# Moving the matmul operands of a 3-block transformer kernel by 32 and 64 bytes in SBUF

## The chip, the cores and the metric

The kernel runs on one core of one Trainium2 chip. The metric is the device time of one execution in microseconds (us); lower is better. SBUF, the on-chip memory, has 128 partitions; an address in this document is a byte or word offset along a partition, the same in all 128. A word is 4 bytes. TensorE multiplies a **moving** operand (up to 512 columns, streamed through) with a **stationary** operand (up to 128 columns, put into the array by a separate weight-load instruction). Both are read from SBUF, and the result is added up in PSUM.

## The reference, cut to what matters

256 tokens of width 2048 pass through three transformer blocks. The projections hold nearly all of the arithmetic:

```
# twice: mixer, then a gated feed-forward (FFN_HIDDEN = 5632)
h = mixer(x @ w_in, ...) @ w_o
x = layer_norm(ALPHA * x + h)
gate, up = jnp.split(x @ w_gu, 2, axis=-1)
x = layer_norm(ALPHA * x + (silu(gate) * up) @ w_d)
# once: neighbourhood + state-space + memory attention, then D_FF = 8192
x = x + rmsnorm(y @ w_out)
x = x + rmsnorm(square(relu(rmsnorm(x) @ w_ff1)) @ w_ff2)
```

All of it is float32. The kernel reaches float32 accuracy with a split: each operand is a high part, rounded to the `float32r` form that TensorE multiplies at a higher rate, plus a low part that holds the rest. A product is then three matmuls: high by high, high by low, low by high.

## The kernel before

**Units.** A weight matrix comes in units of 1024 words for each partition (512 KB). Each lands in one of 8 slots of `weights_raw` (or in a place in the large buffer), ScalarE copies its high part to a slot of `weights_hi` (L294), VectorE subtracts and writes the low part to `weights_lo` (L313), and TensorE uses it. There are 4 slots in each of the two, and one more of each in the large buffer (`hi_at[4]`, `lo_at[4]`).

**Matmuls.** In `block_mm` (L353 to L355) the weights are the moving operand, 512 columns at a time, and the activations are the stationary one, 128 tokens at a time. For each 128 rows of the weight matrix and each of the two token blocks, three matmuls follow one another:

```
nc.tensor.matmul(o, ah, wh, start=(k + j == 0), stop=False)
nc.tensor.matmul(o, ah, wl, start=False, stop=False)
last = nc.tensor.matmul(o, al, wh, start=False, stop=(k + j == kts - 1))
```

The first argument after the output is the stationary operand, the second the moving one. `ah` and `al` are slices of `act_hi`/`act_lo` (all the projections from the model width) or of `hid_hi`/`hid_lo` (the down projections). The same triple stands at L3972 to L3974 (gated feed-forward: here some activations lie in the large buffer, rows "weights_hi,big"), at L693 to L695, L608 to L610 and L580 to L582. Names in the profile's rows are in the order output<-moving,stationary. `narrow_mm` (L382 to L384) has the roles turned round: 16 or 72 weight columns are stationary and 256 tokens of `act_hi`/`act_lo` move. Small attention products (L1046, L3666 and others) and transposes by an identity (L413) are plain float32.

**Addresses.** `build` lays all of SBUF out by hand, in words: `weights_hi` at 8192, `weights_lo` at 12288, `x` at 16384, and from `SCR` = 20480 on `act_hi`, `act_lo`, `hid_hi`, `hid_lo`. `scr(...)` gives other views of those last four, used in other stages. Behind them stand `ident`, `smalls` and the large buffer `BIG`, of which `big(...)` gives views by offset. Every weight slot, every 512-column half of one, and every 128-column slice of the activations begins a multiple of 128 words after that layout's start. So in every triple the stationary and the moving operand have the same address modulo 512 bytes.

**Order.** The order of the work on every engine is written out by hand. Semaphores order the engines: `lo_ready` lets TensorE use a unit, `w_used` gives a slot of the split weights back, and a load into a raw slot waits for `lo_ready` of the unit that was there.

Of the kernel before, what the change touches and what calls it, by code (L numbers as in the profile page):

```python
# [19 lines left out]
F32R = mybir.dt.float32r  # L20
I32 = mybir.dt.int32
# [4 lines left out]
P = 128  # L26
TOK = 256
TT = TOK // P
D = 2048
KT_D = D // P  # L30
# [147 lines left out]
def build(nc, A, out, upto=99):  # L178
# [4 lines left out]
    def at(name, word, shape, dt=F32):  # L183
        assert base + 4 * (word + int(np.prod(shape[1:]))) <= nc.sbuf_usable_end, name
        return nc.alloc_sbuf_tensor_at(name, shape, dt, offset=base + 4 * word)
# [7 lines left out]
    w_lo = at("weights_lo", 12288, [P, SPLIT_SLOTS, UNIT], F32R)  # L193
    x = at("x", 16384, [P, TT, D])
    SCR = 20480
    aT_hi = at("act_hi", SCR, [P, KT_D, TOK], F32R)
    aT_lo = at("act_lo", SCR + 4096, [P, KT_D, TOK], F32R)
    hT_hi = at("hid_hi", SCR + 8192, [P, 8, TOK], F32R)
    hT_lo = at("hid_lo", SCR + 10240, [P, 8, TOK], F32R)
    CON = SCR + 12288  # L200
    ident = at("ident", CON, [P, P])
    smalls = at("smalls", CON + 128, [P, 128])
    BIG = CON + 256
    BIG_END = 53200
    n_view = [0]

    def scr(off, shape, dt=F32):
        n_view[0] += 1
        assert off + int(np.prod(shape[1:])) <= 12288
        return at(f"scratch_{n_view[0]}", SCR + off, shape, dt)  # L210

    def big(off, shape, dt=F32):
        n_view[0] += 1
        assert BIG + off + int(np.prod(shape[1:])) <= BIG_END
        return at(f"big_{n_view[0]}", BIG + off, shape, dt)
# [547 lines left out]
    gdec = big(19856, [P, 16])  # L763
    restart = big(17152, [P, 1024])
    dil_mask = big(18176, [P, 1152])
    chunk_pred = big(20048, [P, P], I32)
    G_Q, G_K, G_V, G_G, G_R, D_Q, D_K, D_V = 0, 512, 1024, 2048, 2064, 3088, 4624, 6160

    ln_vec = [[big(o, [P, D]), big(o + D, [P, D])] for o in (12544, 10752, 10912, 10240)]
# [165 lines left out]
    b_glu = big(18432, [P, 512])  # L935
    mlp_post = big(2048, [P, D])
    dump = scr(8192, [P, TT, D])
    still = scr(8192, [P, P])
    GJ = 32
    T4 = 4  # L940
# [14 lines left out]
    dmat = big(18432, [P, 16, T4 * 16])  # L955
    u4x = big(8192, [P, 16, 2, NCH])
    ux = scr(8192, [NCH, GJ, T4, 16])
    hs = scr(8192, [P, NCH, 2, GJ])
    y4 = big(8192, [NCH, 4, T4, P])
# [3203 lines left out]
def program(nc, shapes, dtypes, upto=99):  # L4163
    aps = {n[3:]: nc.dram_tensor(n, shapes[n], dtypes[n], kind="ExternalInput").ap() for n in shapes}
    out = nc.dram_tensor("out_x", (1, TOK, D), F32, kind="ExternalOutput").ap()
    build(nc, aps, out, upto)
# [86 lines left out]
```

How the kernel before makes its waits and increments, by code:

```python
    def slot_load(sp, c, slot, src, cols, unit):  # L262
        nk = src.shape[1]
        if slot in c.user:
            sp.wait_ge(lo_ready, c.until(c.user[slot] + 1))
        sp.dma_start(raw_at[slot][:, :nk * cols].rearrange("p (k n) -> p k n", n=cols), src).then_inc(landed[slot], 16)
        c.n[f"raw{slot}"] += 1
        c.use(slot, unit)
# [7 lines left out]
    def unit_hi(act, c, size):  # L277
        slot = c.raw_slot()
        act.wait_ge(landed[slot], c.now(f"raw{slot}", 1, 1, 16))
        c.n[f"raw{slot}"] += 1
        high_part(act, c, raw_at[slot], size)
# [1 line left out]
    def high_part(act, c, of, size):  # L285
        to = c.split_slot()
        if to in c.user:
            act.wait_ge(w_used, c.until(c.user[to] + 1))
        done = 0
        if c.n["unit"] == 0:
            done = UNIT // 2
            nc.scalar.copy(hi_at[to][:, :done], of[:, :done]).then_inc(ready("tile_high"), 1)
        nc.scalar.copy(hi_at[to][:, done:size], of[:, done:size]).then_inc(hi_ready, 1)
        c.use(to, c.n["unit"])
        c.n["split"] += 1
        c.n["unit"] += 1
# [5 lines left out]
    def low_part(dve, c, of, size):  # L303
        to = c.split_slot()
        done = 0
        if c.n["unit"] == 0:
            done = UNIT // 2
            dve.wait_ge(ready("tile_high"), 1)
            nc.vector.tensor_tensor(lo_at[to][:, :done], of[:, :done], hi_at[to][:, :done].bitcast(F32),
                                    ALU.subtract).then_inc(ready("tile_low"), 1)
        dve.wait_ge(hi_ready, c.now("unit", 1))
```

## Time and profile before

| | |
|---|---|
| median of 3 runs | 3403.22 us (3403.2 to 3405.02) |
| the profiled execution's own time | 3405.52 us |
| its span, from the first to the last instruction | 3403.7 us |
| TensorE (matmul) busy | 3387.6 us, 100% of the span |
| granted TensorE clock, mean | 0.999 of full speed |
| matmul records | 15664 |
| VectorE, ScalarE busy | 2225.6 us (65%), 1737.9 us (51%) |
| HBM traffic | 184 GB/s over the span |

The span is 1.8 us shorter than the execution's own time. Matmul records overlap: one lasts longer than the distance from its start to the start of the next. So the rate of TensorE is read from starts, not from durations.

### The profile page before, as it was taken

Reading aid. Unit: us, or ns where it says so; the run is one execution under the profiler, and the core shown is the slowest. Engines: PE = TensorE matmul, PEld = TensorE weight load, DVE = VectorE, ACT = ScalarE, POOL = GpSimd, SP = SyncE. Lnnn points to the kernel's source line nnn. Section 1 sums busy time; section 2 is a strip of 40 time slices with the busy share of each in tenths; the row PEclk is TensorE's granted clock in tenths of the full one; section 3 lists DMA queues with packets and bytes.
Section 4 is the critical chain, followed back from the end, with each engine's and each line's share of the span. In section 5 each row is a group of like instructions: output and inputs, shape, how many; then the busy total and the mean of one; then the engine's idle time right before and its main releaser. Section 6 shows DMA issues by size and latency. Waiting matters only on the chain.

```text
span 3403.7 us, 41843 instructions
## 1 busy us (share of the span) xinstructions
PE 3387.6 (100%) x15664; PEld 2774.5 (82%) x15664; DVE 2225.6 (65%) x2428; ACT 1737.9 (51%) x2211; POOL 302.4 (9%) x418
## 2 busy tenths in 40 slices
PE   9999999999999999999999999999999999999998
PEld 8788878888888887777888878888888788888887
DVE  4544477888887755666556545557544887777776
ACT  5444445555554455454444434446546665555553
POOL 0000000000000000002343303000281000000000
PEclk9999999999999999999999999999999999999999
DMA  7556555665666465456666657665654466665654
GB/s 246 170 167 182 192 185 180 210 211 173 213 210 205 148 185 156 126 196 170 188 186 196 189 161 211 212 194 172 181 182 147 143 223 198 198 197 195 196 186 130
DMA packets 333339, 630.42 MB, mean 185 GB/s; under 512 B 33180, under 2 KB 36096, under 8 KB 331648
## 3 DMA queue, kind: packets, MB, share of 16 engines
q1 hardware_dynamic: 326272, 603.20, 56.5%
q0 software_dynamic: 6768, 25.05, 2.3%
q8 instruction: 102, 1.67, 0.2%
q14 instruction: 53, 0.43, 0.0%
q10 hardware_dynamic: 144, 0.07, 0.0%
HBM read 624.86 MB, written 2.33 MB: 184 GB/s over the span
## 4 chain that ended last, share of the span: by engine, by line
PE 96%; DVE 2%; ACT 1%; DMA 0%; issue 0%; SPq 0%; DVEq 0%; ACTq 0%
PE psum L353 23%; PE psum L355 22%; PE psum L354 22%; PE psum L3974 6%; PE psum L3972 6%; PE psum L3973 6%; PE psum L413 3%; PE psum L693 1%; PE psum L1046 1%; PE psum L695 1%; PE psum L694 1%; DVE weights_lo L313 1%; PE psum L1059 0%; PE psum L3869 0%; PE psum L610 0%; PE psum L608 0%
## 5 line engine op out<-in xcount | busy, mean ns | idle before, releaser
L313 DVE TENSOR_TENSOR weights_lo<-weights_raw,weights_hi 128x1024 fp32r<-128x1024 f32 (+1 forms) x1069 | 1315.2, 1239 | 932.4 <-ACT weights_hi L294 926.9
L294 ACT CAST weights_hi<-weights_raw 128x1024 fp32r<-128x1024 f32 (+1 forms) x1069 | 1118.9, 1049 | 1351.6 <-PE psum L355 1163.3
L353 PE MATMUL psum<-weights_hi,act_hi 128*128 128x512 f32 x2088 | 834.0, 399 | 0.2
L355 PE MATMUL psum<-weights_hi,act_lo 128*128 128x512 f32 x2088 | 815.8, 391 | 0.0
L354 PE MATMUL psum<-weights_lo,act_hi 128*128 128x512 f32 x2088 | 814.1, 390 | 0.0
L353 PE MATMUL psum<-weights_hi,hid_hi 128*128 128x512 f32 x1192 | 467.6, 392 | 0.2 <-DVE big L3214 0.2
L355 PE MATMUL psum<-weights_hi,hid_lo 128*128 128x512 f32 x1192 | 464.3, 389 | 0.0
L354 PE MATMUL psum<-weights_lo,hid_hi 128*128 128x512 f32 x1192 | 463.9, 389 | 0.0
L353 PEld LDWEIGHTS psum<-weights_hi,act_hi 128*128 128x128 f32 x2088 | 392.7, 188 | 86.0 <-issue 8.9
L355 PEld LDWEIGHTS psum<-weights_hi,act_lo 128*128 128x128 f32 x2088 | 392.3, 188 | 84.7
L354 PEld LDWEIGHTS psum<-weights_lo,act_hi 128*128 128x128 f32 x2088 | 393.1, 188 | 76.4
L353 PEld LDWEIGHTS psum<-weights_hi,hid_hi 128*128 128x128 f32 x1192 | 223.8, 188 | 48.7 <-issue 2.7
L355 PEld LDWEIGHTS psum<-weights_hi,hid_lo 128*128 128x128 f32 x1192 | 223.7, 188 | 47.1
L354 PEld LDWEIGHTS psum<-weights_lo,hid_hi 128*128 128x128 f32 x1192 | 223.9, 188 | 45.5
L3972 PE MATMUL psum<-weights_hi,act_hi 128*128 128x512 f32 x478 | 187.4, 392 | 0.0
L3974 PE MATMUL psum<-weights_hi,act_lo 128*128 128x512 f32 x478 | 186.3, 390 | 0.0
L3973 PE MATMUL psum<-weights_lo,act_hi 128*128 128x512 f32 x478 | 186.0, 389 | 0.0
L294 ACT CAST big<-weights_raw 128x1024 fp32r<-128x1024 f32 x100 | 105.3, 1053 | 92.0 <-PE psum L3974 47.3
L313 DVE TENSOR_TENSOR big<-weights_raw,big 128x1024 fp32r<-128x1024 f32 x100 | 122.2, 1222 | 32.7 <-ACT big L294 32.4
L413 PE MATMUL psum<-ident,big 128*128 128x128 f32 (+1 forms) x754 | 117.3, 272 | 0.2 <-DVE hid_lo L430 0.2
L413 PEld LDWEIGHTS psum<-ident,big 128*128 128x128 f32 (+1 forms) x754 | 93.4, 139 | 28.9 <-issue 3.5
L2391 DVE TENSOR_TENSOR x<-x,psum 128x1024 f32<-128x1024 f32 x54 | 65.8, 1219 | 60.4 <-PE psum L355 60.4
(523 smaller groups left out, 3751.3 us busy)
## 6 DMA issues: line engine op xcount, KB each, us to landing
weights_raw<-in_ffn_wgu SPq DMA_DIRECT2D x312, 512.0 KB, 4.0
weights_raw<-in_w_ff SPq DMA_DIRECT2D x224, 512.0 KB, 4.7
weights_raw<-in_ffn_wd SPq DMA_DIRECT2D x176, 512.0 KB, 4.4
weights_raw<-in_even_w_in SPq DMA_DIRECT2D x120, 512.0 KB, 3.6
weights_raw<-in_w_in SPq DMA_DIRECT2D x64, 512.0 KB, 3.8
weights_raw<-in_odd_w_in SPq DMA_DIRECT2D x60, 512.0 KB, 3.7
big<-in_ffn_wgu SPq DMA_DIRECT2D x32, 512.0 KB, 8.1
weights_raw<-in_odd_w_o SPq DMA_DIRECT2D x32, 512.0 KB, 3.7
```

The lines of the kernel that those rows point to most:

```text
L294: nc.scalar.copy(hi_at[to][:, done:size], of[:, done:size]).then_inc(hi_ready, 1)
L313: nc.vector.tensor_tensor(lo_at[to][:, done:size], of[:, done:size], hi_at[to][:, done:size].bitcast(F32), ALU.subtract).then_inc(lo_ready, 1)
L353: nc.tensor.matmul(o, ah, wh, start=(k + j == 0), stop=False)
L354: nc.tensor.matmul(o, ah, wl, start=False, stop=False)
L355: last = nc.tensor.matmul(o, al, wh, start=False, stop=(k + j == kts - 1))
L413: last = nc.tensor.transpose(psum[:w, 4 + t % 2, at_col:at_col + p], src, ident[:p, :p])
L693: nc.tensor.matmul(o, ah, wh, start=(u + j == 0), stop=False)
L694: nc.tensor.matmul(o, ah, wl, start=False, stop=False)
L2391: return TENS(o, o, s, ALU.add)
L3972: nc.tensor.matmul(at_bank(b), ah, wh, start=start_, stop=False, skip_group_check=True)
L3973: nc.tensor.matmul(at_bank(b), ah, wl, start=False, stop=False, skip_group_check=True)
L3974: last = nc.tensor.matmul(at_bank(b), al, wh, start=False, stop=stop, skip_group_check=True)
```

## The change

Offsets in SBUF, and nothing else. `act_hi` moves up by 8 words (32 bytes). `act_lo`, `hid_hi`, `hid_lo`, `ident`, `smalls`, the whole large buffer and the views of `scr` move up by 16 words (64 bytes). The weight slots (`weights_raw`, `weights_hi`, `weights_lo`) and `x` stay. `chunk_pred`, a mask in the large buffer, takes an offset 144 words lower so that the buffer still ends inside SBUF. No instruction is added, removed or put in another place; the sequence on every engine is the same.

```diff
-    aT_hi = at("act_hi", SCR, [P, KT_D, TOK], F32R)
-    aT_lo = at("act_lo", SCR + 4096, [P, KT_D, TOK], F32R)
-    hT_hi = at("hid_hi", SCR + 8192, [P, 8, TOK], F32R)
-    hT_lo = at("hid_lo", SCR + 10240, [P, 8, TOK], F32R)
-    CON = SCR + 12288
+    aT_hi = at("act_hi", SCR + 8, [P, KT_D, TOK], F32R)
+    aT_lo = at("act_lo", SCR + 4096 + 16, [P, KT_D, TOK], F32R)
+    hT_hi = at("hid_hi", SCR + 8192 + 16, [P, 8, TOK], F32R)
+    hT_lo = at("hid_lo", SCR + 10240 + 16, [P, 8, TOK], F32R)
+    CON = SCR + 12288 + 16
     ident = at("ident", CON, [P, P])
     smalls = at("smalls", CON + 128, [P, 128])
     BIG = CON + 256
@@
-        return at(f"scratch_{n_view[0]}", SCR + off, shape, dt)
+        return at(f"scratch_{n_view[0]}", SCR + 16 + off, shape, dt)
@@
-    chunk_pred = big(20048, [P, P], I32)
+    chunk_pred = big(19904, [P, P], I32)
```

After the change the stationary operand stands 32 bytes (`act_hi`) or 64 bytes (`act_lo`, `hid_hi`, `hid_lo`, activations in the large buffer) further than the moving one, modulo 512 bytes, where the moving one is a slot of `weights_hi` or `weights_lo`. Where the moving operand is the weight slot in the large buffer, it moves too: against `hid_hi`, `hid_lo`, `act_lo` and `big` the distance stays 0, against `act_hi` it becomes -32 bytes. In `narrow_mm` the moving operand (`act_hi`, `act_lo`) moves and the stationary one stays.

## Rows read from the trace of the kernel before

**Rows 1.** The page: busy time, TensorE's clock in 40 slices, the chain by engine.

```profile
PE 3387.6 (100%) x15664; PEld 2774.5 (82%) x15664; DVE 2225.6 (65%) x2428; ACT 1737.9 (51%) x2211; POOL 302.4 (9%) x418
...
PEclk9999999999999999999999999999999999999999
...
PE 96%; DVE 2%; ACT 1%; DMA 0%; issue 0%; SPq 0%; DVEq 0%; ACTq 0%
```

**Rows 2.** Matmul groups by line and shape: count, busy us, mean ns of one, idle before.

```profile
L353 PE MATMUL psum<-weights_hi,act_hi 128*128 128x512 f32 x2088 | 834.0, 399 | 0.2
...
L353 PE MATMUL psum<-weights_hi,hid_hi 128*128 128x512 f32 x1192 | 467.6, 392 | 0.2 <-DVE big L3214 0.2
...
L3972 PE MATMUL psum<-weights_hi,act_hi 128*128 128x512 f32 x478 | 187.4, 392 | 0.0
...
L3972 PE MATMUL psum<-weights_hi,big 128*128 128x512 f32 x222 | 88.7, 400 | 0.0
...
L353 PE MATMUL psum<-big,hid_hi 128*128 128x512 f32 x128 | 49.9, 390 | 0.0
...
L3972 PE MATMUL psum<-big,act_hi 128*128 128x512 f32 x122 | 47.7, 391 | 0.0
...
L3972 PE MATMUL psum<-big,big 128*128 128x512 f32 x78 | 30.7, 394 | 0.0
...
L3666 PE MATMUL psum<-big,big 128*128 128x256 f32 x24 | 5.8, 380 | 0.0
```

**Rows 3.** Timeline, TensorE, us from 297: start and duration of single matmuls.

```profile
297.13 0.39 PE L353 MATMUL psum<-weights_hi,act_hi 128*128 128x512 f32 x1
...
310.73 0.39 PE L353 MATMUL psum<-weights_hi,act_hi 128*128 128x512 f32 x1
```

**Rows 4.** Timeline, TensorE, us 221 to 225, behind and ahead of transposes.

```profile
221.86 0.40 PE L354 MATMUL psum<-weights_lo,act_hi 128*128 128x512 f32 x1
222.09 0.40 PE L355 MATMUL psum<-weights_hi,act_lo 128*128 128x512 f32 x1
222.32 0.40 PE L353 MATMUL psum<-weights_hi,act_hi 128*128 128x512 f32 x1
222.56 0.39 PE L354 MATMUL psum<-weights_lo,act_hi 128*128 128x512 f32 x1
222.78 0.39 PE L355 MATMUL psum<-weights_hi,act_lo 128*128 128x512 f32 x1
...
223.94 0.39 PE L354 MATMUL psum<-weights_lo,act_hi 128*128 128x512 f32 x1
...
224.40 0.60 PE L413 MATMUL psum<-ident,big 128*128 128x128 f32 x4
```

**Rows 5.** Weight loads by line and shape: count, busy us, mean ns, idle before.

```profile
L353 PEld LDWEIGHTS psum<-weights_hi,act_hi 128*128 128x128 f32 x2088 | 392.7, 188 | 86.0 <-issue 8.9 <-DVE weights_lo L313 0.9
...
L382 PEld LDWEIGHTS psum<-act_hi,weights_hi 128*72 128x72 f32 x16 | 2.3, 141 | 0.0
...
L382 PEld LDWEIGHTS psum<-act_hi,weights_hi 128*16 128x16 f32 x16 | 1.5, 94 | 0.4
```

**Rows 6.** Timeline, TensorE, us 56 to 60: `narrow_mm` with 16 stationary columns.

```profile
56.01 0.28 PE L382 MATMUL psum<-act_hi,weights_hi 128*16 128x256 f32 x1
...
59.88 0.28 PE L382 MATMUL psum<-act_hi,weights_hi 128*16 128x256 f32 x1
```

**Rows 7.** Timeline, weight loads, at us 297.

```profile
297.13 0.19 PEld L354 LDWEIGHTS psum<-weights_lo,act_hi 128*128 128x128 f32 x1
```

**Rows 8.** Timeline, TensorE, us 327: plain float32 matmuls of 256 columns.

```profile
327.71 1.46 PE L3666 MATMUL psum<-big,big 128*128 128x256 f32 x6
```

**Rows 9.** Waits: who waited for whom, us in total, times, longest.

```profile
ACT weights_hi L294 <- PE psum L355: 1203.7, 746, 6.3
```

**Rows 10.** DMA issues: count, KB each, median us from issue to landing.

```profile
weights_raw<-in_ffn_wgu SPq DMA_DIRECT2D x312, 512.0 KB, 4.0
...
big<-in_ffn_wgu SPq DMA_DIRECT2D x32, 512.0 KB, 8.1
```

## The prediction

> **What bounds the kernel now.** I read the page first. TensorE is busy for the whole span, its clock is granted in full in every slice, and the chain that ended last is TensorE for 96% [rows 1]. So a change of the time has to be a change of TensorE's rate, or a new wait. Next comes what it does. The groups by line show three equal rows for every triple (high by high, high by low, low by high), of which one stands here: 2088 + 1192 + 478 + 222 + 128 + 122 + 78 = 4308, times 3 is 12,924 matmuls of 512 columns [rows 2]. A few smaller groups of the same kind I leave out. The durations of 389 to 400 ns say nothing about the rate, since one matmul starts before the last has ended. The timeline gives it: from the L353 at 297.13 to the L353 at 310.73 lie 20 triples, 60 starts, in 13.60 us [rows 3]. That is 226.7 ns for each matmul, and 12,924 x 0.2267 = 2930 us, 86% of the span.
>
> At 2.4 GHz, one column a cycle, 512 columns are 213.3 ns. So each matmul pays 13.4 ns on top, 173 us in all. Whatever these 13.4 ns are, the change can act on nothing else: TensorE has no idle time worth naming, and no instruction moves.
>
> **What the change can touch.** It changes addresses alone. The term is 12,924 times the change of one interval, so 0.53 ns for each matmul is already 6.8 us, the 0.2% that a measurement of this kernel can tell from no change. The question is whether the 13.4 ns come from two reads of SBUF that stand in each other's way: the stream of the moving operand, and the weight load for the next matmul. The two do overlap: the matmul L353 starts at 297.13, and the weight load for the following L354 starts at 297.13 as well [rows 3, 7]. And before the change both start at the same address modulo 512 bytes.
>
> *For a collision.* The interval isn't a constant. Behind a group of transposes it goes 0.23, 0.23, 0.24, 0.22 us, and from 221.86 to 223.94 nine starts take 2.08 us, 231.1 ns each, before it settles at 226.7 [rows 3, 4]. The operands are of the same kind in both stretches, so the same work costs 4.4 ns more or less by how loads and streams lie in time. A plain float32 matmul of 256 columns, which takes two cycles for each column and so also streams for 213.3 ns, has less on top: six of them last 1.46 us, and less the last one's own 0.380 that is 1.08 / 5 = 216 ns [rows 2, 8]. It reads SBUF at half the rate and would have room for a second reader.
>
> *Against a collision that the address decides.* In `narrow_mm` the moving side is again `float32r`, 256 columns, ideally 106.7 ns. Between 56.01 and 59.88 lie 33 starts in 3.87 us, 117.3 ns each [rows 6]. The load there is 16 columns, an eighth of a full one, and the slices are 64 bytes apart, so that the distance between the two operands runs through eight values modulo 512 bytes. The cost on top is still 10.6 ns. So at most 13.4 - 10.6 = 2.8 ns of the 13.4 go with the size of the load, and over those eight distances the pace keeps even to what the timeline resolves. Second, the two reads don't run side by side. A load lasts 94, 141 and 188 ns for 16, 72 and 128 columns [rows 5], which is (188 - 94) / 112 = 0.84 ns a column, against 226.7 / 512 = 0.44 for the stream. While the load walks through its 512 bytes, the stream walks through some 1000, so the distance between them sweeps through about 500 bytes in every matmul. A shift of 32 or 64 bytes moves the point in the sweep where they meet, not how often they do.
>
> So I take 0 for the term, and keep as its bounds -10.7 ns (down to the 216 of the plain float32 matmul) and +4.4 ns (up to the 231.1 behind the transposes), for each of 12,924 matmuls: -138 us and +57 us.
>
> The Trainium skill ("SBUF — State Buffer", section "Who interferes with whom") says that TensorE reads the moving operand and the weight load through two independent ports, and that PE and ACT never wait on anyone. By that rule the term is 0 as well. The same page ("Specifications") names lines of 16 bytes; 32 and 64 are multiples of 16, so no operand would touch more lines than before. But the skill ("TensorE: Matmul & The Clock Gate", section "Back-to-back issue gap") gives N / 2.4 + 2.5 ns for a warm matmul, 215.8 for 512 columns, and the trace's 226.7 doesn't agree; if the change brought the interval to that figure, the time would be an estimated 141 us shorter. No run here says yet where the difference comes from.
>
> **The rest of the edits** I cost at nothing. The views in `big` and `scr` that VectorE, ScalarE and GpSimd use move by 64 bytes; VectorE is busy for 65% and ScalarE for 51% [rows 1], and ScalarE waits 1203.7 us in 746 waits, 1.6 each, for TensorE to give weight slots back [rows 9]. That slack hides some tenths more on an instruction. Units that land in the large buffer take 8.1 us against 4.0 in a raw slot [rows 10]; both ways they are issued ahead, and if the new destination made one slower by those 4 us again, ScalarE's slack would be gone for that unit: 32 such units and at worst 4 - 1.6 = 2.4 us each, 77 us. I see nothing that would do it, since the size and the shape of each transfer stay.
>
> The sum is 0 on the profiled execution, whose own time is 3405.5 for a span of 3403.7, 2.3 above the median of the runs. Against that median I forecast 3403.
>
> **The rivals.**
>
> *A, faster: the distance between the operands matters.* The part that goes with the load, 2.8 ns, would vanish: 12,924 x 2.8 = 36 us, 3367 us. If the whole excess over 216 were a collision, it would be 3265. For it: the interval answers to fine timing [rows 3, 4], and in every triple the distance was exactly 0 before, the one value of which a sweep can't be shown to be harmless, for no full-width load at another distance stands beside a `float32r` stream in the groups. Against it: `narrow_mm` and the sweep. 0.32 for this side, most of it near the small end.
>
> *B, slower: the settled rhythm is lost.* The stream settles at 226.7 with load and stream starting together [rows 3, 7]. With other addresses the meeting point lies elsewhere, and high and low stationary operands now differ from one another (32 and 64 bytes), so that the triple may not settle and stays at the 231.1 seen behind transposes [rows 4]. That is 12,924 x 4.4 = 57 us, 3460. Half of it, if only one of the three in a triple and its neighbour suffer, is 3432. It decides as soon as the mean interval grows by 0.53 ns. Against it: that it needs the same sensitivity to addresses as A, and then in the worse direction. 0.18.
>
> *C, the change does nothing,* because the 13.4 ns belong to each `float32r` matmul whatever its addresses are: my forecast, 0.50, with a range of its own of 3400 to 3408.
>
> **How the numbers follow.** C is the likeliest and gives 3403. A reaches down to 3265, B up to 3460. I let the range end at 3350, which holds A's small form and leaves some 0.12 below it, and at 3425, which holds a B of 1.7 ns a matmul and leaves some 0.07 above. Faster by over 0.2% is A, 0.32; within 0.2% is C, 0.50; slower by over 0.2% is B, 0.18.
>
> **What the changed kernel's profile would show.** If I am right: the same 60 starts of L353 to L355 in 13.60 us, the same 33 starts of L382 in 3.87, the same duration of weight loads, 188 ns. If A: fewer than 13.57 us for 60 starts of rows with `weights_hi` against `act_hi` and `hid_hi`, while the rows "big,hid_hi" [rows 2], in which both operands move by 64 bytes, stay at 226.7; that difference would prove the distance and not the address. If B: more than 13.63 us, and the uneven steps of [rows 4] all through a block. I would be wrong also if the weight loads themselves changed their length, or if a wait for a DMA into the large buffer appeared in the chain.

## The result: slower by 1.7%

The changed kernel takes 3462.88 us (median of 4 runs, 3462.34 to 3463.4) against 3403.89 us for the kernel before in the same comparison (3403.2 to 3405.02): 59.0 us more, a ratio of 1.0173 with a 95% interval of 1.0155 to 1.0191. The forecast was no change.

The page of the profiled execution after the change, its head, the busy line, TensorE's clock and the chain by engine:

```profile
span 3460.9 us, 41843 instructions
...
PE 3446.1 (100%) x15664; PEld 2772.1 (80%) x15664; DVE 2225.5 (64%) x2428; ACT 1736.1 (50%) x2211; POOL 302.1 (9%) x418
...
PEclk9999999999999999999999999999999999999999
...
PE 98%; DVE 1%; ACT 1%; issue 0%; DVEq 0%; POOL 0%; ACTq 0%; POOLq 0%
```

Beside [rows 1] nothing has moved but TensorE: the same 15,664 matmuls at the same clock, granted in full, take 57 us more of the span (3460.9 against 3403.7), and VectorE, ScalarE and the weight loads are as busy as before. So the loss is TensorE's pace. The timeline of TensorE after the change: `narrow_mm`, which answers to [rows 6], the stretch that answers to [rows 3] (`act_hi`, `act_lo` stationary), and one with `hid_hi`, `hid_lo`:

```profile
56.25 0.28 PE L382 MATMUL psum<-act_hi,weights_hi 128*16 128x256 f32 x1
...
60.10 0.28 PE L382 MATMUL psum<-act_hi,weights_hi 128*16 128x256 f32 x1
...
297.24 0.39 PE L355 MATMUL psum<-weights_hi,act_lo 128*128 128x512 f32 x1
...
311.12 0.39 PE L355 MATMUL psum<-weights_hi,act_lo 128*128 128x512 f32 x1
...
709.50 0.39 PE L353 MATMUL psum<-weights_hi,hid_hi 128*128 128x512 f32 x1
...
716.50 0.39 PE L353 MATMUL psum<-weights_hi,hid_hi 128*128 128x512 f32 x1
```

From the first row to the second of a stretch, 60 starts take 13.88 us, 231.3 ns each, where they took 13.60 before [rows 3]. In the down projection 30 starts take 7.00 us, 233.3 ns each. `narrow_mm` keeps its pace: 33 starts in 3.85 us, 3.87 before [rows 6]. The matmul groups by line of the changed kernel:

```profile
L353 PE MATMUL psum<-weights_hi,act_hi 128*128 128x512 f32 x2088 | 839.0, 402 | 0.1
...
L353 PE MATMUL psum<-weights_hi,hid_hi 128*128 128x512 f32 x1192 | 473.3, 397 | 0.0
...
L353 PE MATMUL psum<-big,hid_hi 128*128 128x512 f32 x128 | 50.1, 391 | 0.0
```

The first two rows grew from 399 and 392 ns [rows 2]. The third, in which both operands moved by 64 bytes, has 391 against 390. A duration isn't a pace, though: by their starts these `hid_hi` matmuls went from 226.7 to 229.0 ns, in the midst of neighbours at a distance of 64 bytes, where the matmuls of `weights_hi` and `weights_lo` against `hid_hi` went from 227.0 to 233.3.

The sum of it: (2088 + 478) x 3 = 7698 matmuls with `act_hi`/`act_lo` and a weight slot x 4.6 ns = 35 us; 1192 x 3 = 3576 with `hid_hi`/`hid_lo` x 6.6 = 24 us; 222 x 3 = 666 with activations in the large buffer x 6.6 = 4 us. That is 63 us by settled paces. Added up from every start in the two traces, the 57.2 us between the spans are 28.0 for `act_hi`/`act_lo` against a weight slot (8177 matmuls, some of them in rows that the sum leaves out), 22.0 for `hid_hi`/`hid_lo` (3624), 3.5 for activations in the large buffer (666) and 3.8 where the moving operand isn't one of the plain weight slots (1176). The other 2020 matmuls, narrow ones, transposes and plain float32, lost 0.0. The first two shares are smaller than by settled paces, since the kernel before wasn't settled everywhere either [rows 4]: its matmuls with `act_hi`/`act_lo` took 227.8 ns on average, not 226.7, leaving out intervals of 250 ns and more.

### The profile page after: what moved, and what is told of

It reads as the page before. It is cut to its first block, busy times and chain, and to the rows that moved or that the text cites. A ratio compares the mean times of both kernels' runs of the same rounds, so it can differ in the third digit from the quotient of the medians.

```text
span 3460.9 us, 41843 instructions
## 1 busy us (share of the span) xinstructions
PE 3446.1 (100%) x15664; PEld 2772.1 (80%) x15664; DVE 2225.5 (64%) x2428; ACT 1736.1 (50%) x2211; POOL 302.1 (9%) x418
## 3 DMA queue, kind: packets, MB, share of 16 engines
q8 instruction: 102, 1.67, 0.2%
## 4 chain that ended last, share of the span: by engine, by line
PE 98%; DVE 1%; ACT 1%; issue 0%; DVEq 0%; POOL 0%; ACTq 0%; POOLq 0%
PE psum L353 23%; PE psum L354 23%; PE psum L355 23%; PE psum L3972 6%; PE psum L3973 6%; PE psum L3974 6%; PE psum L413 3%; PE psum L693 1%; PE psum L1046 1%; PE psum L694 1%; PE psum L695 1%; PE psum L610 0%; PE psum L609 0%; PE psum L608 0%; PE psum L1059 0%; PE psum L3869 0%
## 5 line engine op out<-in xcount | busy, mean ns | idle before, releaser
L354 PE MATMUL psum<-weights_lo,act_hi 128*128 128x512 f32 x2088 | 823.2, 394 | 0.0
L3973 PE MATMUL psum<-weights_lo,act_hi 128*128 128x512 f32 x478 | 188.2, 394 | 0.0
```

What stands on the lines that cost most here:

```text
L3973: nc.tensor.matmul(at_bank(b), ah, wl, start=False, stop=False, skip_group_check=True)
```

## The experiments

The theory that I set out with: the distance between the stationary and the moving operand, modulo some power of two, sets the pace of a `float32r` matmul. The rivals: the move of the activations or of the large buffer counts by itself (other alignment for transfers or for the other engines); or high and low operands at two distances keep the triple from settling.

### Everything moved together (all_moved), and one distance for all (apart_32, apart_64, apart_96)

All four in one comparison, in which the kernel before took 3403.35 us (9 runs). all_moved keeps the offsets of before and moves the start of the whole layout:

```diff
-    base = -(-nc.sbuf_base // 64) * 64
+    base = -(-nc.sbuf_base // 64) * 64 + 64
...
-    chunk_pred = big(20048, [P, P], I32)
+    chunk_pred = big(19904, [P, P], I32)
```

The other three are the change with one number N (8, 16 or 24 words) in all its places; apart_96 also lets the layout end 8 words later:

```diff
-    aT_hi = at("act_hi", SCR, [P, KT_D, TOK], F32R)
-    aT_lo = at("act_lo", SCR + 4096, [P, KT_D, TOK], F32R)
+    aT_hi = at("act_hi", SCR + N, [P, KT_D, TOK], F32R)
+    aT_lo = at("act_lo", SCR + 4096 + N, [P, KT_D, TOK], F32R)
...
-    CON = SCR + 12288
+    CON = SCR + 12288 + N
```

> Every tensor in SBUF moves up by 64 bytes, the weight slots too, so every address differs from the kernel before but every distance between a stationary and a moving operand is what it was, 0 modulo 512 bytes. Distance theory (the distance between the operands sets the pace of a float32r matmul): 3403 us, settled interval 226.7 ns. Address theory (where the activations, the scratch views or the large buffer lie, by themselves, sets the time): 3463 us, settled interval near 233 ns.

> All that stands behind the weight slots and x (activations, scratch views, constants, large buffer) is 32 bytes further; one distance for high and low operands alike. Distance theory: rows with distance 32 take some 230.6 ns, as the matmuls of the change whose own and next stationary operand both stand at 32 do, so 12,300 x 3.9 ns = 48 us more than before, 3451 us. Mixture theory (the triple can't settle because high and low operands stand at different distances, 32 and 64): one distance settles at 226.7, 3403 us.

> As apart_32, with 64 bytes for everything. Distance theory: all rows go like the hid rows of the change, 233.3 ns, so 12,300 x 6.6 ns = 81 us more than before, 3484 us, slower than the change itself. Mixture theory: 3403 us.

> As apart_32, with 96 bytes for everything. Distance theory has no number for 96 from the two traces: slower than before if 0 is a special point, and between 226.7 and 236 ns for a matmul, so 3403 to 3520 us. Mixture theory: 3403 us.

| kernel | distance of the activations from the weight slots | median, us (runs) | ratio, 95% interval |
|---|---|---|---|
| all_moved | 0 | 3404.65 (8) | 1.0003 (0.9991 to 1.0014) |
| apart_32 | 32 bytes | 3473.42 (2) | 1.0205 (1.0176 to 1.0235) |
| apart_64 | 64 bytes | 3475.08 (2) | 1.021 (1.018 to 1.024) |
| apart_96 | 96 bytes | 3482.99 (2) | 1.0233 (1.0204 to 1.0263) |

The timeline of TensorE in apart_64, behind the first starts of a block:

```profile
300.18 0.39 PE L355 MATMUL psum<-weights_hi,act_lo 128*128 128x512 f32 x1
...
311.38 0.39 PE L355 MATMUL psum<-weights_hi,act_lo 128*128 128x512 f32 x1
```

48 starts in 11.20 us are 233.3 ns each. Every address in all_moved is new, 64 bytes higher, and it costs nothing, so the new addresses by themselves are out. One distance for high and low alike costs more than the two of the change, so the mixture is out too, and the forecast's own reason for the slow rival with it. The distance theory stands, but its number for 32 bytes was wrong: I had read 230.6 ns from those matmuls of the change that stand among neighbours at 64, and a kernel all at 32 runs at 233.2 on average. A pace belongs to a sequence of distances, not to one matmul. For apart_64 I had expected 81 us more and it was 72: the settled 6.6 ns were taken for every matmul, though not all of them ran at 226.7 before.

### A map of the distance (distance_map)

A kernel of its own, which leaves out the whole computation and only issues matmuls from data at rest, while all the other engines are idle (a cut of it; the comments are added here):

```
            for i in range(reps // 3):
                k = i % 2
                ah, al = hi[:, 128 * k:128 * k + width], lo[:, 256 + 128 * k:256 + 128 * k + width]
                wh, wl = w[:, 0:cols], w[:, 512:512 + cols]
                mm(ah, wh, cols, width)
                mm(ah, wl, cols, width)
                last = mm(al, wh, cols, width)
...
        for g in GAPS:            # 0, 8, 16, 32, 48, 64, 96, ... 480, 496 bytes
            part(still[g], still[g], moving)
```

> Not the reference's computation: this kernel leaves all of it out and only issues matmuls. 20 groups of 96 float32r matmuls of 512 columns, in the same triples as the kernel before, each group behind four plain float32 matmuls; within a group the stationary operands stand at one distance from the moving ones modulo 512 bytes, from 0 to 496. Then the pair of distances of the change (high 32, low 64), loads of 16 and 64 columns at distances 0 and 64, matmuls of 256 columns at 0 and 64, and bf16 at 0, 64 and 256. Distance theory: group 0 takes 226.7 ns a matmul once settled (96 in 21.9 us), groups 32 and 64 some 233 (22.5 us), group 96 some 234. A variant in which memory is split in banks by a few low address bits: the pace repeats with a period (64, 128 or 256 bytes) and is 226.7 again there. A variant in which only the same address is special: every other distance takes 230 ns or more. If the stream and the load collide at all, loads of 16 columns lose less with the distance than loads of 128, and bf16 matmuls, which read half the bytes, show no difference between the distances and come nearer to 213.3.

Its timeline on TensorE, one row for a group of 96 matmuls: start, then the time from the first start to the last end. The name of the stationary operand says the distance.

```profile
137.47 22.64 PE L72 MATMUL psum<-moving,gap064b 128*128 128x512 f32 x96
...
184.13 22.55 PE L72 MATMUL psum<-moving,gap128b 128*128 128x512 f32 x96
...
230.62 22.23 PE L72 MATMUL psum<-moving,gap192b 128*128 128x512 f32 x96
...
276.79 22.05 PE L72 MATMUL psum<-moving,gap256b 128*128 128x512 f32 x96
...
322.77 22.65 PE L72 MATMUL psum<-moving,gap320b 128*128 128x512 f32 x96
...
369.44 22.55 PE L72 MATMUL psum<-moving,gap384b 128*128 128x512 f32 x96
...
415.92 22.23 PE L72 MATMUL psum<-moving,gap448b 128*128 128x512 f32 x96
...
508.00 22.43 PE L72 MATMUL psum<-moving,gap000b 128*16 128x512 f32 x96
...
531.08 22.48 PE L72 MATMUL psum<-moving,gap064b 128*16 128x512 f32 x96
...
600.39 11.76 PE L72 MATMUL psum<-moving,gap000b 128*128 128x256 f32 x96
...
612.80 11.55 PE L72 MATMUL psum<-moving,gap064b 128*128 128x256 f32 x96
...
625.08 20.88 PE L72 MATMUL psum<-moving_b,bf000b 128*128 128x512 bf16 x96
646.69 20.88 PE L72 MATMUL psum<-moving_b,bf064b 128*128 128x512 bf16 x96
```

To read a pace off a row, take away the last one's own 0.39 us and divide by the 95 intervals: 22.05 gives 228.0 ns, 22.64 gives 234.2. The first starts of a group weigh in there. The settled pace, from the starts of the last 48 matmuls of a group in the trace, by the distance modulo 256 bytes:

| distance, bytes | 0 | 32 | 64 | 96 | 128 | 160 | 192 | 224 | 240 |
|---|---|---|---|---|---|---|---|---|---|
| settled ns | 226.7 | 233.3 | 233.3 | 234.3 | 232.4 | 233.3 | 228.9 | 233.3 | 228.3 |

The pairs 64 and 320, 128 and 384, 192 and 448 are equal to within 0.01 us in 22: over the 20 distances tried the pace repeats after 256 bytes. 0 (and 256) is the best of the 20 distances. The paces agree with the kernel's, 226.7 at 0 and 233.3 at 64, with the other engines at rest, so VectorE, ScalarE and the transfers have no part in it. bf16 takes 215.8 ns settled at each of its three distances, the rows are alike to 0.01 us; so of the two types only `float32r` shows the effect. Whether its twice as many bytes are the reason isn't shown: its weight loads last longer too, 193 ns against 98 for bf16, and plain float32 is in no map. With loads of 16 columns the distance hardly counts, 231.1 ns at 0 and 231.7 at 64. That much was expected. Two things weren't. With loads of 16 columns instead of 128, distance 0 takes 231.1 ns, more than with full loads. And with 256 moving columns distance 0 is the slower one: 120.0 ns settled against 117.8 at 64.

### The map tried on the kernel (acts_first_minus_64)

The map says that 64 bytes the other way cost less. The activations are laid out ahead of the weight slots, and all behind them moves:

```diff
-    w_hi = at("weights_hi", 8192, [P, SPLIT_SLOTS, UNIT], F32R)
-    w_lo = at("weights_lo", 12288, [P, SPLIT_SLOTS, UNIT], F32R)
-    x = at("x", 16384, [P, TT, D])
-    SCR = 20480
+    SCR = 8192
+    w_hi = at("weights_hi", SCR + 12288 + 16, [P, SPLIT_SLOTS, UNIT], F32R)
+    w_lo = at("weights_lo", SCR + 16384 + 16, [P, SPLIT_SLOTS, UNIT], F32R)
+    x = at("x", SCR + 20480 + 16, [P, TT, D])
...
-    CON = SCR + 12288
+    CON = SCR + 24576 + 16
```

> All of the kernel before, with the activations laid out ahead of the weight slots and the weight slots, x and the rest 64 bytes further: the activations now stand at distance -64 (192 modulo 256) from the weight slots. Distance theory with the period of 256 bytes from the distance map: 228.9 ns a matmul at 192 against 226.7 at 0, on some 12,000 matmuls, so 27 us more than before, 3430 us. If any distance but 0 costs the same, whatever its sign: 3463 to 3483 us, as for +32 to +96.

3424.81 us, ratio 1.0062 (1.0045 to 1.0079): 21.9 us slower than before, where the map gave 27 and a rule "any distance but 0" 60 to 80. Its timeline on TensorE:

```profile
299.60 0.39 PE L353 MATMUL psum<-weights_hi,act_hi 128*128 128x512 f32 x1
...
310.59 0.39 PE L353 MATMUL psum<-weights_hi,act_hi 128*128 128x512 f32 x1
```

48 starts in 10.99 us, 229.0 ns each, as at 192 in the map. Over all intervals under 250 ns, the unsettled ones behind transposes with them, the mean of the 12,361 matmuls at this distance is 229.2 ns against 227.6 in the kernel before: some 1.7 ns and 21 us. The 27 came from settled paces alone, which the kernel before didn't hold throughout.

### The large buffer alone (buffer_only)

```diff
-    CON = SCR + 12288
+    CON = SCR + 12288 + 16
...
-    chunk_pred = big(20048, [P, P], I32)
+    chunk_pred = big(19904, [P, P], I32)
```

> Of the change only the constants and the large buffer move, by 64 bytes; activations and scratch views stay. Distance theory: distance 64 for the 666 matmuls whose activations lie in the large buffer and whose weights don't, 6 ns each, 4 us; distance -64 for some 750 whose weights lie there and whose activations don't, 2 ns each, 1.5 us; 3409 us in all. If the move of the large buffer costs by itself (transfers, VectorE, ScalarE, GpSimd at another alignment), it takes a good part of the change's 59 us: above 3415.

3413.14 us, ratio 1.003 (1.0019 to 1.0042): 10.2 us, where I had 5.5. The starts in its trace say where they go, intervals under 250 ns alone: 641 matmuls at distance 64 take 233.1 ns on average, 872 at -64 take 230.6, and 11,726 at distance 0 take 227.9, where the same took 227.8, 227.5 and 227.6 in the kernel before. 641 x 5.3 + 872 x 3.0 + 11,726 x 0.3 = 3.4 + 2.6 + 3.5 = 9.5 us. The third term is what I left out: a few matmuls at another distance also unsettle those behind them. All of it lies in the 2626 that come within 24 matmuls behind one at another distance, 228.6 ns against 227.2; the other 9100 keep their 227.7. Under 1 us is left for transfers or other engines.

### Finer distances, pairs, widths (finer_map)

The same kernel as distance_map with other groups; again it leaves the computation out. A group is given by where its operands start:

```
# name: (bytes of the high operand, of the low one, of the high weights, of the low weights, moving columns, stationary columns)
...
"gap252": (252, 252, 0, 0, 512, 128),
...
"hi32lo64": (32, 64, 0, 0, 512, 128),
...
"both64": (64, 64, 64, 64, 512, 128),
...
"cols384gap0": (0, 0, 0, 0, 384, 128),
...
```

> Not the reference's computation: it is left out, only matmuls are issued, 37 groups of 96 in the triples of the kernel before. Distances of 4 to 252 bytes in between those of the distance map; high and low operands at two distances; weights that start at other addresses; loads of 16, 64 and 96 columns; 256, 384 and 448 moving columns. Distance theory: distances 240, 248 and 252 lie like 496 did, between 226.7 and 229 ns; weights and operands that both stand at 64 or both at 128 take 226.7 as at 0; of the pairs, high 32 with low 64 takes some 231.5 ns, as the change's rows do. If every line of a load costs the stream a fixed time, the cost on top of the ideal falls with the width of the load and stays when the moving columns become fewer: 384 columns 173 ns and 448 columns 200 ns at distance 0. If stream and load lock to each other's rhythm instead, the cost goes up and down with the moving columns and the width with no such order, and no pair or distance is below 226.7.

Some rows of its timeline on TensorE:

```profile
104.59 22.18 PE L86 MATMUL psum<-from0b,at_gap240b 128*128 128x512 f32 x96
...
150.71 22.65 PE L86 MATMUL psum<-from0b,at_gap252b 128*128 128x512 f32 x96
...
243.29 22.45 PE L86 MATMUL psum<-from0b,at_hi32lo64b 128*128 128x512 f32 x96
...
428.20 22.05 PE L86 MATMUL psum<-from0b,at_hi0lo240b 128*128 128x512 f32 x96
450.90 22.64 PE L86 MATMUL psum<-from0b,at_hi240lo0b 128*128 128x512 f32 x96
...
704.49 22.33 PE L86 MATMUL psum<-from0b,at_wide96gap0b 128*96 128x512 f32 x96
...
727.47 22.18 PE L86 MATMUL psum<-from0b,at_wide96gap64b 128*96 128x512 f32 x96
...
750.29 16.91 PE L86 MATMUL psum<-from0b,at_cols384gap0b 128*128 128x384 f32 x96
...
826.36 11.76 PE L86 MATMUL psum<-from0b,at_cols256gap0b 128*128 128x256 f32 x96
```

- The change's pair, high 32 and low 64, settles at 231.1 ns, which is the 231.3 of the changed kernel.
- Weights and operands both at 64, or both at 128, take 226.7: it is the distance.
- One word is enough to lose it: 252 bytes give 233.3 and 4 bytes 232.4, 248 gives 233.3; only 240 (228.3) and 192 are near. I had expected 248 and 252 to lie near 0.
- Which operand stands where counts: high 0 with low 240 takes 226.7, high 240 with low 0 takes 233.3.
- At distance 0 the cost over one column a cycle is 13.3 ns for 256 columns (120.0), 384 (173.3) and 512 alike, 16.0 for 448. It doesn't grow with the columns. With loads of 16, 64 and 96 columns, distance 0 takes 231.1, 230.0 and 230.0 for 512 columns, and only the full 128 take 226.7. So it isn't a fixed price for each line of a load either. I had expected 200 ns for 448 columns and found 202.7.
- Distance 0 is not the best for every shape. With 512 columns and loads of 96, distance 64 takes 228.3 ns against 230.0; with loads of 64, distance 192 takes 228.3 against 230.0; with full loads and 448 columns, distance 64 takes 202.2 against 202.7; with 256 columns, 128 takes 118.8 and 64 takes 117.8 (distance_map) against 120.0. With 384 columns 0 is the better, 173.3 against 176.7 at 64.
- The settled paces take few values. Of the 139 groups in the three maps with 512 columns and full loads, 62 are at 226.7, 228.3, 230.0, 231.7, 233.3 or 235.0, in steps of 1.67 ns, which is four cycles of 2.4 GHz; 38 are at 231.1 and nine at 228.9, between those steps, as the mean over a longer pattern would be. That it is such a mean is my reading and isn't shown.

### Together or own, and 80 random layouts (own_or_together)

The last of these kernels, the computation left out again, 60 matmuls a group. A group lists where the moving and the stationary operand of each matmul of a cycle start:

```
("together64", [(0, 64), (64, 0)]),    # each load at distance 0 from the stream of the matmul before
("own64", [(0, 0), (64, 64)]),         # each matmul's own two operands at distance 0
```

> Not the reference's computation: only matmuls are issued, 93 groups of 60. In the groups named together, each weight load has distance 0 to the stream that runs while it loads, and 64, 128 or 192 to the stream of its own matmul; in the groups named own it is the other way round. Theory of the simultaneous reads: the together groups take 226.7 ns a matmul as at distance 0, the own groups 229 to 233. Rival, that the distance between a matmul's own two operands counts: the own groups take 226.7. The 80 other groups are triples with three distances drawn at random (high operand, low operand, low weights): if 226.7 is the floor, none is below it and nearly all are above; a group below would be a better layout than that of the kernel before.

```profile
38.49 14.16 PE L162 MATMUL psum<-moving,own64b 128*128 128x512 f32 x60
53.29 14.05 PE L162 MATMUL psum<-moving,together128b 128*128 128x512 f32 x60
68.00 13.96 PE L162 MATMUL psum<-moving,own128b 128*128 128x512 f32 x60
...
112.18 13.88 PE L162 MATMUL psum<-moving,allzero2b 128*128 128x512 f32 x60
```

Both theories fall in this form. Settled, together takes 233.3, 230.0 and 231.7 ns at 64, 128 and 192, own takes 231.4, 228.3 and 231.5, and only the group with everything at 0 takes 226.7. (The settled pace is here that of the last 36 matmuls.) But the groups tell less than I meant them to. A load starts with the matmul before its own [rows 3, 7], and a matmul's record lasts 0.39 us, longer than an interval of 0.23, so by the records the load overlaps two streams; in the together groups of two these start at different addresses. A load that meets both isn't ruled out. What is shown is that neither distance alone sets the pace. Of the 80 random layouts none is below 228.9 ns, 75 are at 230.0 or above, and 28 at 231.1. The layout of the kernel before sits at the lowest pace of the 139 groups with 512 columns and full loads; the only one with unequal addresses (modulo 256) that ties with it is high 0, low 240. So the maps hold no better layout for this kernel.

## Why the prediction was wrong

- **Right:** the bound and the form of the term. TensorE's pace sets the time, the term is the number of 512-column matmuls times the change of one interval, and 0.5 ns decides. The smaller groups left out of the 12,924 bring it to 13,643. Transfers, the large buffer and the other engines cost nothing by themselves (all_moved, buffer_only).
- **The step that failed:** "A shift of 32 or 64 bytes moves the point in the sweep where they meet, not how often they do", and from it "So I take 0 for the term". The term is +4.6 ns where `act_hi` and `act_lo` are stationary and +6.6 in the down projections, settled; over all starts it is 3.4 and 6.1. The sweep counted meetings as if load and stream ran on at their own rates. The evenly repeating 226.7 of [rows 3] and the uneven starts of [rows 4] spoke against it: the sequence settles into a rhythm. The maps show that where the operands start decides into which. I had cited these rows for a collision and then let an average argue them away.
- **The other reason against a collision, from `narrow_mm`, was weak as well:** "at most 13.4 - 10.6 = 2.8 ns of the 13.4 go with the size of the load". It compared 256 columns and a load of 16 with 512 and 128. With full loads 256 columns cost 13.3 on top (finer_map), and a load of 16 under 512 columns costs 4.4 ns more than a full one (distance_map). Neither size orders the cost, so no split of it could be read from `narrow_mm`. Nor could its eight distances stand for those of a full load: under 512 columns a load of 16 changes the pace by 0.6 ns between distance 0 and 64, 128 or 192, a full load by up to 6.7 (both maps). The rows themselves did what I said: L382 keeps its pace in the changed kernel.
- **Rival B was what happened, at its price:** 57 us and 3460 forecast, 59 and 3463 measured. That the numbers lie so close is partly luck: the 4.4 ns for every matmul became 3.4 on 8177 and 6.1 on 3624, by the starts. Its bound, the unsettled 231.1 of [rows 4], is close to the 231.3 to which the changed triple settles, and below the 233.3 of the down projections. Its reason was wrong: high and low operands at different distances aren't the trouble, since 32 for both and 64 for both are slower still (apart_32, apart_64). I gave it 0.18 and left it outside the range, for want of a row at another distance. The sign that I gave for A, the rows "big,hid_hi" keeping 226.7, didn't hold either: they went to 229.0. A bound worked out from rows on the measured kernel was set aside for an argument about rates.
- **The rules of the Trainium skill:** that TensorE's two read ports are independent and that it never waits ("SBUF — State Buffer", "Who interferes with whom") speaks for no change. The runs don't agree for `float32r`, whose pace moves by up to 8.9 ns a matmul with where the two operands start, and show nothing against it for bf16. The gap of N / 2.4 + 2.5 ns that the Trainium skill gives ("TensorE: Matmul & The Clock Gate", "Back-to-back issue gap") fits bf16 at 215.8 and misses `float32r` by 10.9.

**What stays open:** how load and stream get in each other's way. The runs show that the pace depends on the starting addresses modulo 256 bytes, on the width of the load and on the columns, and that neither the distance to the stream of the matmul before nor the one to the matmul's own moving operand explains it alone. That load and stream get in each other's way at all is my reading: the runs show the effect of their addresses, not the wait itself. Nor is it shown what the other 10.9 ns over bf16 are, which no layout removed. A distance of 256 bytes was tried in the map and not in the kernel itself, whose layout has no room for it.

## What to carry to other kernels

In a stream of `float32r` matmuls of 512 columns with a full load of 128 for each, let all stationary and moving slices start at the same address modulo 256 bytes: the best case here, and a stray 32 bytes cost 2% of a kernel that is 86% such matmuls. Don't carry the rule to other shapes without measuring: with 256 or 448 columns, or loads of 64 or 96, another distance was the faster one. When a trace shows one kind of instruction at two paces, take both as the bounds for any change of what it reads, and don't average the difference away. Thirty groups of bare matmuls in one small kernel settle such a question in under a millisecond of chip time, which no argument from rates could.

## What the runs showed of the hardware that I had not expected

- `float32r` matmuls of 512 columns run settled at 226.7 to 235.6 ns, with full loads, depending on where their operands start (226.7 at 0; 235.6 in one of the own groups, whose middle matmul of three stood at 64); bf16 ones at 215.8 at all three distances tried.
- A narrower weight load can make the stream slower: 226.7 ns with 128 stationary columns, 231.1 with 16, both at distance 0.
- With 256 moving columns equal addresses are the slower choice: 120.0 ns at distance 0, 117.8 at 64.
- The distance counts to the word: 0 gives 226.7, 252 bytes give 233.3, 4 give 232.4, 240 give 228.3.
